# First projection of a hybrid encoder: blocks 1 to 5 as three products of split operands, with a group of loads moved on ScalarE's queue

## The chip, the cores and the metric

The program runs on one core of one Trainium2 chip. The metric is the device time of one execution in microseconds (us), median of several runs. TensorE (PE) multiplies, VectorE (DVE) and ScalarE (ACT) work element by element, GpSimd (POOL) does some of that too, and SyncE (SP) issues most transfers. Each engine works off its own instructions in order and meets the others at semaphores. A DMA that ACT issues takes time in ACT's own queue of instructions.

## What is computed

Two layers over T = 272 tokens (16 learned meta tokens and 256 given ones) of width 1024. The part that matters here is the start of layer 0:

```python
proj = rmsnorm(h, norm_mix_even[i]) @ w_in_ab[i]
ssd_out = ssd_mixer(proj[..., :o0], proj[..., o0:o1], proj[..., o1:o2],
                    ssd_conv_w[i], ssd_conv_b[i], ssd_a_log[i], ssd_dt_bias[i],
                    ssd_d[i], ssd_norm_w[i])
...
attn_out = diff_attention(proj[..., o2:], cos, sin, diff_lambda[i],
                          diff_subln_w[i], lambda_init)
h = h + jnp.concatenate([ssd_out, attn_out], axis=-1) @ w_out_ab[i]
```

In `ssd_mixer` a depthwise convolution over 5 tokens and a SiLU follow the projection, then a state-space scan in both directions. Behind it come a dense SwiGLU, a long convolution (Hyena) whose filter is a small network with sines, and a mixture of eight SwiGLU experts, which is most of the time.

## The kernel before

Everything is kept transposed: a tile is 128 output channels by 272 tokens in one of eight PSUM banks. The program has no scheduler. Each engine's instructions are written out by hand in their order, and `ORDER` numbers the PSUM tiles: a tile may be opened when the tile eight numbers before it has been read (`used_...`), and `tile_ready` counts the tiles that are closed.

The normalised input is `xn` (8 pieces of 128x272, fp32, written by DVE). The weights come in blocks of 256 columns (128x2048 numbers, 1 MB) through a ring of four slots. SP issues the first two at the start, and each later one when the last tile of the block four before it is closed. Block n of the projection gives tiles proj 2n and proj 2n+1. `linear` multiplies a block in plain fp32, 8 matmuls for each tile; the trace has two records for each such matmul.

PE's order is: blocks 0 (while `xn` comes), the transposed parameters, block 1, the 48 small matmuls of `dt`, blocks 2 and 3, filter layer 0 (`fw1`), block 4, filter layer 1 (`fw23`), block 5, filter layer 2, then cumulative sums (`cs`), transposes, and the head loop of the scan with blocks 6 to 9 in it. A filter layer k > 0 waits for the sine of layer k-1.

ACT copies each tile of blocks 0 to 3 to `xp`, applies the SiLU after the convolution (`ssd_silu`), and before tile 4 it takes the exp and log of `dt`. DVE makes one convolution for each of these eight tiles, 5 instructions (L1098, and L1034 four times), with the `dt` rows ahead of the fifth; then the arguments of the three sines (`filter_argument`, L1105 to L1110), which ACT's `filter_sine` (L707) waits for. From 85 us the head loop runs, in which DVE is busy without a pause.

Behind the input's transposes ACT issues five loads for `dt` and then eight more: the rest of the constant table `ktab`, `sel8` twice, `zpos`, `fw1`, `fw23` twice and the router. GpSimd's products W1 (L582) and DVE's masks need the table, PE's filter layers the small ones (`filter_in`).

Later stages (from the SwiGLU on, line 1236 and 815 for the splits) already use split operands: a number is x = hi + lo, with hi its copy rounded to fp32r (`ring_high` on ACT, `ring_low` on DVE for a block), and a product is three matmuls in fp32r:

```python
def product(o, hi, lo, moving, start, stop):
    mm(o, hi, moving[0], start, False)
    mm(o, hi, moving[1], False, False)
    return mm(o, lo, moving[0], False, stop)
```

Of the kernel before, what the change touches and what calls it, by code (L numbers as in the profile page):

```python
# [251 lines left out]
def trunk(nc, A, out):  # L252
    ctx = ExitStack()
    with ctx:
# [50 lines left out]
        ring_hi, ring_lo = overlay("ring_hi", 13600, 2, SLOT), overlay("ring_lo", arena_n, RING, SLOT)  # L305
        ring_hi2 = overlay("ring_hi2", 14864, 2, 256 * KT)
# [150 lines left out]

        def high_of(n, k):
            return ring_hi[:, n % 2, 0:256 * k] if n < B_HY else ring_hi2[:, (n + 1) % 2, 0:256 * k]

# [155 lines left out]
        def _(act):  # L616
# [57 lines left out]
            act.dma_start(ktab[:, K_FIRST:], A["k_table"][:, K_FIRST:]).then_inc(sem("table_in"), 16)  # L674
            for r in (0, 32):
                act.dma_start(sel8[r:r + HEADS, :], A["k_sel8"]).then_inc(sem("table_in"), 16)
            act.dma_start(zpos[:], A["k_zpos"]).then_inc(sem("filter_in"), 16)
            act.dma_start(fw1[:], A["hy_f_w1"][0]).then_inc(sem("filter_in"), 16)
            act.dma_start(fw23[:, 0, :], A["hy_f_w2"][0]).then_inc(sem("filter_in"), 16)
            act.dma_start(fw23[:, 1, :], A["hy_f_w3"][0]).then_inc(sem("filter_in"), 16)  # L680
            act.dma_start(router[:], A["moe_router"][0].rearrange("(k p) n -> p k n", p=P)).then_inc(sem("router_in"), 16)
# [8 lines left out]
            for j in range(8):  # L690
                if j == 4:

                    act.wait_ge(sem("dt_raw"), 1)
                    act.wait_ge(sem("dt_in"), 16 * 5)
                    a(nc.scalar.activation(dtw[:, 7, 0:16], a_log, ACT.Exp))
                    a(nc.scalar.activation(dtw[:, 2, :], dtw[:, 1, :], ACT.Exp, scale=-1.0))
                    a(nc.scalar.activation(dtw[:, 3, :], dtw[:, 2, :], ACT.Ln, bias=1.0), sem("dt_log"))
                copy("proj", j, xp[:, j, 2:2 + T])
                if j == 0:
                    parameters()  # L700
                if j >= 1:
                    ssd_silu(j - 1)
# [108 lines left out]

            def ring_high(n, i=0, k=KT):

                act.wait_ge(slot_in[n % RING], 16 * (n // RING + 1) + 16 * i)
                nc.scalar.activation(high_of(n, k), ring[:, n % RING, 0:256 * k], ACT.Copy).then_inc(sem("ring_high"), 1)  # L815

# [212 lines left out]
        def _(dve):  # L1029
# [37 lines left out]
            V.memset(crd[:, 7:8], 0.0).then_inc(used("ss1"), 1)  # L1067
            dve.wait_ge(used("param"), 1)
# [12 lines left out]
            for j in range(8):  # L1081
# [17 lines left out]
                for k in range(1, CONV):  # L1099
                    mult_add(c, xp[:, j, k:k + T], w(k), c, sem("conv_ready") if k == CONV - 1 else None)  # L1100
            def filter_argument(k):

                t = ready(dve, "mlp", k)
                x0, x1, x2 = harg[0:64, 0, :], harg[0:64, 1, :], harg[0:64, 2, :]
                v(V.tensor_scalar(x0, t[0:64, 0:ZT], par[0:64, C_FV + k:C_FV + k + 1], par[0:64, C_FV + 3 + k:C_FV + 4 + k], ALU.add, ALU.mult), used("mlp"))  # L1105
                v(V.tensor_scalar(x1, x0, 1.0 / (2.0 * math.pi), ROUND, ALU.mult, ALU.add))
                v(V.tensor_scalar(x1, x1, ROUND, None, ALU.subtract))
                mult_add(x0, x1, -TWO_PI_A, x0)
                mult_add(x2, x1, -TWO_PI_B, x0)
                v(V.tensor_scalar(x1, x2, 3.1415925, -3.1415925, ALU.min, ALU.max), sem("arg_ready"))  # L1110
# [120 lines left out]
            def ring_low(n, i=0, k=KT):  # L1231

                dve.wait_ge(sem("ring_high"), n - B_FF + 1 + 4 * i)
                c = slice(0, 256 * k)
                high = high_of(n, k)
                V.tensor_tensor(ring_lo[:, n % RING, c], ring[:, n % RING, c], high.bitcast(F32), ALU.subtract).then_inc(sem("ring_split"), 1)  # L1236

# [4 lines left out]
            def split_norm(col, s):  # L1242

                for k in range(KT + 1):
# [3 lines left out]
                    if k >= 1:  # L1248
                        dve.wait_ge(sem("xn_high"), KT + k)
                        V.tensor_tensor(xn_lo[:, k - 1, :], xn[:, k - 1, :], xn_hi[:, k - 1, :].bitcast(F32), ALU.subtract).then_inc(sem(s), 1)  # L1250

            def weighted_low(k, col):
                dve.wait_ge(sem("xn_high"), k + 1)
                V.scalar_tensor_tensor(out=xn_lo[:, k, :], in0=hT[:, k, :], scalar=par[:, col + k:col + k + 1], in1=xn_hi[:, k, :].bitcast(F32),
                                       op0=ALU.mult, op1=ALU.subtract).then_inc(sem("xn2_ready"), 1)
# [340 lines left out]
        def _(pe):  # L1596
# [25 lines left out]

            def turn(o, src, n=P):
# [71 lines left out]
            for n in range(6):  # L1695
                linear("proj", 2 * n, n, xn, coming=sem("xn1_ready") if n == 0 else None)
# [171 lines left out]
            def swiglu_columns(i, c, first=False):  # L1868

                for part in range(2):  # L1870
                    n = B_FF + 2 * c + part
                    pe.wait_ge(sem("ring_split"), 2 * c + part + 1 + 4 * i)
# [25 lines left out]
            for b in range(4):  # L1898
                for half in range(2):
                    n = B_DN + 2 * b + half  # L1900
                    pe.wait_ge(sem("ring_split"), n - B_FF + 1)
# [51 lines left out]
            def in_columns(i, b):  # L1953

                n = B_HY + b
                pe.wait_ge(sem("ring_split"), n - B_FF + 1 + 4 * i)
# [237 lines left out]
```

## Time and profile before

| | us |
|---|---|
| median of 3 runs (1646.52 to 1650.33) | 1646.89 |
| the profiled execution | 1656.01 |
| its span, first to last instruction | 1654.2 |
| PE busy in the span | 1614.9 (98%) |
| DVE busy | 1244.3 (75%) |
| ACT busy | 976.6 (59%) |

The profile is of one execution, which took 9.1 us more than the median of the runs. Busy times are sums over the span; which engine sets the end has to be read from the chain of waits and, for one stage, from the timelines of that stage. TensorE's clock has two levels, 1.2 and 2.4 GHz, and the column PEclk gives what was granted as a share of the higher one.

### The profile page before, as it was taken

What the parts mean: (1) busy time and instruction counts of PE and PEld (TensorE: products, weight loads), DVE (VectorE), ACT (ScalarE), POOL (GpSimd) and SP (SyncE); (2) the same over time, 40 slices, a digit from 0 to 9 for tenths busy, and PEclk for the clock granted to TensorE, in tenths of its full rate; (3) what the DMA queues carried; (4) which work ended last, traced back from release to release, by engine and by line L of the source; (5) the groups of instructions that cost most, each with busy time, mean ns of one, the idle gap of its engine ahead of it and who ended that gap; (6) DMA issues with size and microseconds to landing.
All of it is one profiled execution on the core that took longest, in us unless ns stands there. A gap on an engine that the chain in (4) does not pass through costs nothing.

```text
span 1654.2 us, 22043 instructions
## 1 busy us (share of the span) xinstructions
PE 1614.9 (98%) x8334; PEld 1350.9 (82%) x8334; DVE 1244.3 (75%) x1184; ACT 976.6 (59%) x885; POOL 77.7 (5%) x87
## 2 busy tenths in 40 slices
PE   8998999999999998999999999999999999999997
PEld 6765699999699587888888888888888888888886
DVE  5488456654647555988988888888888988988984
ACT  3274344433356124777677677677677677677773
POOL 0250000000302400000000000000000000000000
PEclk9999999999989997999999999999999999999998
DMA  8322145567125144999999999999999999999991
GB/s 279 102 79 75 48 143 170 174 195 213 52 86 169 52 153 141 372 375 332 355 370 339 356 370 340 356 372 337 356 372 337 357 373 336 355 375 332 355 369 66
DMA packets 221126, 429.60 MB, mean 260 GB/s; under 512 B 9514, under 2 KB 76592, under 8 KB 220752
## 3 DMA queue, kind: packets, MB, share of 16 engines
q1 hardware_dynamic: 217816, 424.82, 72.7%
q10 hardware_dynamic: 3256, 4.06, 0.7%
q8 instruction: 34, 0.56, 0.1%
q14 instruction: 20, 0.16, 0.0%
HBM read 427.80 MB, written 1.05 MB: 259 GB/s over the span
## 4 chain that ended last, share of the span: by engine, by line
PE 90%; DVE 5%; DMA 2%; ACT 1%; issue 1%; SPq 0%; DVEq 0%; ACTq 0%
PE ps L1612 87%; PE ps L1624 3%; DVE arena L1034 1%; DMA ring<-in_ffn_w_down_dram 1%; DMA raw<-in_moe_w_up_dram 1%; DVE arena L1137 0%; DVE ring_lo L1236 0%; DVE arena L1148 0%; DVE arena L1142 0%; DVE arena L1149 0%; ACT w_hi L925 0%; ACT ring_hi L815 0%; DMA raw<-in_moe_w_gate_dram 0%; DVE arena L1170 0%; DVE arena L1143 0%
## 5 line engine op out<-in xcount | busy, mean ns | idle before, releaser
L1400 DVE TENSOR_TENSOR w_lo<-raw,w_hi 128x2048 fp32r<-128x2048 f32 x224 | 511.9, 2290 | 82.4 <-ACT w_hi L925 81.4
L925 ACT ACTIVATE w_hi<-raw 128x2048 fp32r<-128x2048 f32 x224 | 429.3, 1919 | 182.0 <-DMA raw<-in_moe_w_up_dram 91.7
L1612 PE MATMUL ps<-w_hi,xg_hi 128*128 128x512 f32 x904 | 358.2, 396 | 4.7 <-DVE w_lo L1580 2.1
L1612 PE MATMUL ps<-w_hi,xg_lo 128*128 128x512 f32 x904 | 353.4, 391 | 0.0
L1612 PE MATMUL ps<-w_lo,xg_hi 128*128 128x512 f32 x904 | 352.7, 390 | 0.0
L1404 DVE TENSOR_TENSOR w_lo<-raw,w_hi 128x2048 fp32r<-128x2048 f32 x110 | 251.6, 2287 | 41.1 <-ACT w_hi L929 40.9
L929 ACT ACTIVATE w_hi<-raw 128x2048 fp32r<-128x2048 f32 x110 | 211.1, 1919 | 77.9 <-DMA raw<-in_moe_w_down_dram 77.5
L1612 PEld LDWEIGHTS ps<-w_hi,xg_hi 128*128 128x128 f32 x904 | 170.2, 188 | 39.3 <-DVE w_lo L1580 2.5
L1612 PEld LDWEIGHTS ps<-w_hi,xg_lo 128*128 128x128 f32 x904 | 169.9, 188 | 36.3
L1612 PEld LDWEIGHTS ps<-w_lo,xg_hi 128*128 128x128 f32 x904 | 170.4, 188 | 33.9
L1612 PE MATMUL ps<-w_hi,eh_hi 128*128 128x512 f32 x440 | 172.8, 393 | 1.7 <-issue 1.7
L1612 PE MATMUL ps<-w_lo,eh_hi 128*128 128x512 f32 x440 | 171.4, 390 | 0.0
L1612 PE MATMUL ps<-w_hi,eh_lo 128*128 128x512 f32 x440 | 171.4, 389 | 0.0
L1612 PE MATMUL ps<-xn_hi,ring_hi 128*128 128x272 f32 x544 | 159.1, 292 | 0.9 <-DVE crd L1348 0.8
L1612 PE MATMUL ps<-xn,ring 128*128 128x272 f32 (+1 forms) x640 | 158.8, 409 | 0.9 <-DVE xn L1034 0.8
L1612 PE MATMUL ps<-xn_hi,ring_lo 128*128 128x272 f32 x544 | 157.8, 290 | 0.0
L1612 PE MATMUL ps<-xn_lo,ring_hi 128*128 128x272 f32 x544 | 157.0, 289 | 0.0
L1236 DVE TENSOR_TENSOR ring_lo<-ring,ring_hi 128x2048 fp32r<-128x2048 f32 (+1 forms) x42 | 102.7, 2445 | 66.9 <-ACT ring_hi L815 66.0
L1612 PEld LDWEIGHTS ps<-xn,ring 128*128 128x128 f32 x640 | 126.8, 200 | 30.6 <-issue 5.3
L815 ACT ACTIVATE ring_hi<-ring 128x2048 fp32r<-128x2048 f32 (+1 forms) x42 | 85.6, 2038 | 72.6 <-PE ps L1612 59.9
L1612 PEld LDWEIGHTS ps<-xn_hi,ring_hi 128*128 128x128 f32 x544 | 103.0, 189 | 1.8 <-DVE crd L1348 0.9
L1612 PEld LDWEIGHTS ps<-xn_lo,ring_hi 128*128 128x128 f32 x544 | 103.1, 190 | 0.1
(289 smaller groups left out, 1920.1 us busy)
## 6 DMA issues: line engine op xcount, KB each, us to landing
raw<-in_moe_w_gate_dram SPq DMA_DIRECT2D x112, 1024.0 KB, 5.2
raw<-in_moe_w_up_dram SPq DMA_DIRECT2D x112, 1024.0 KB, 5.3
raw<-in_moe_w_down_dram SPq DMA_DIRECT2D x112, 1024.0 KB, 5.1
ring<-in_w_in_ab_dram SPq DMA_DIRECT2D x12, 1024.0 KB, 6.6
ring<-in_hy_w_in_dram SPq DMA_DIRECT2D x12, 1024.0 KB, 5.1
ring<-in_ffn_w_gate_dram SPq DMA_DIRECT2D x11, 1024.0 KB, 5.3
ring<-in_ffn_w_up_dram SPq DMA_DIRECT2D x11, 1024.0 KB, 5.3
ring<-in_ffn_w_down_dram SPq DMA_DIRECT2D x8, 1408.0 KB, 7.2
```

Source lines behind the costliest of these rows:

```text
L815: nc.scalar.activation(high_of(n, k), ring[:, n % RING, 0:256 * k], ACT.Copy).then_inc(sem("ring_high"), 1)
L925: nc.scalar.activation(w_hi[:, j, :], raw[:, j, :], ACT.Copy).then_inc(sem("gu_high"), 1)
L929: nc.scalar.activation(w_hi[:, 4 + j, :], raw[:, 4 + j, :], ACT.Copy).then_inc(sem("d_high"), 1)
L1034: v(V.scalar_tensor_tensor(out=out_, in0=in0, scalar=scalar, in1=in1, op0=op0, op1=op1), s)
L1236: V.tensor_tensor(ring_lo[:, n % RING, c], ring[:, n % RING, c], high.bitcast(F32), ALU.subtract).then_inc(sem("ring_split"), 1)
L1400: V.tensor_tensor(w_lo[:, j, :], raw[:, j, :], w_hi[:, j, :].bitcast(F32), ALU.subtract).then_inc(sem("gu_split"), 1)
L1404: V.tensor_tensor(w_lo[:, 4 + j, :], raw[:, 4 + j, :], w_hi[:, 4 + j, :].bitcast(F32), ALU.subtract).then_inc(sem("d_split"), 1)
L1612: return nc.tensor.matmul(o, l, r, start=start, stop=stop)
L1624: return nc.tensor.transpose(o, src, ident[0:n, 0:n])
```

## The change

Blocks 1 to 5 of the first projection are multiplied as three fp32r products instead of one fp32 product; block 0 stays as it is. For this ACT makes hi copies of the eight pieces of `xn` and of each block, and DVE the differences. The hi copies of blocks go to three buffers in turn (`ring_hi0`), the copies of `xn` to `xn0_hi` and `xn0_lo`. The copy and the difference of block 1 stand right behind those of `xn`; the copies of blocks 2 to 5 stand on ACT behind tiles 0, 2, 4 and 6, the differences on DVE behind convolutions 0, 2, 4 and 6. The eight later loads move on ACT's queue from ahead of the first tile's copy to behind the second tile's copy (`later_loads`). The counts of the semaphores that later stages share are adapted.

```diff
--- before.py
+++ after.py
@@ -303,6 +303,9 @@
         ring_hi, ring_lo = overlay("ring_hi", 13600, 2, SLOT), overlay("ring_lo", arena_n, RING, SLOT)
+        ring_hi0 = [overlay(f"ring_hi0{i}", at, 2048) for i, at in enumerate((5472, 7520, 20064))]
+        xn0_hi, xn0_lo = overlay("xn0_hi", 13056, KT, T), overlay("xn0_lo", 15232, KT, T)
         ring_hi2 = overlay("ring_hi2", 14864, 2, 256 * KT)
         ffh_hi, ffh_lo = overlay("ffh_hi", 0, FFT, T), overlay("ffh_lo", 5984, FFT, T)
         xn_hi, xn_lo = overlay("xn_hi", 19232, KT, T), overlay("xn_lo", 21408, KT, T)
@@ -455,8 +458,15 @@
                 return ("down", (n - B_DN) // 2 * 2 + (n - B_DN) % 2)
             return ("hy", 2 * (n - B_HY) + 1) if n < B_HO else ("ho", 2 * (n - B_HO) + 1)
+        EARLY = 5
         def high_of(n, k):
+            if n <= EARLY:
+                return ring_hi0[n % 3][:, 0:256 * k]
             return ring_hi[:, n % 2, 0:256 * k] if n < B_HY else ring_hi2[:, (n + 1) % 2, 0:256 * k]
+        def split_number(n):
+            return n if n <= EARLY else EARLY + n - B_FF + 1
         slot_in = [sem(f"slot{i}_in") for i in range(RING)]
@@ -671,14 +681,25 @@
             act.dma_start(a_log, A["ssd_a_log"].rearrange("e a h -> e (a h)").partition_broadcast(P)).then_inc(sem("dt_in"), 16)
             act.dma_start(lam_in, A["diff_lambda"].rearrange("e a h -> e (a h)").partition_broadcast(P)).then_inc(sem("dt_in"), 16)
             act.dma_start(d_in, A["ssd_d"].rearrange("e a h -> e (a h)").partition_broadcast(P)).then_inc(sem("dt_in"), 16)
-            act.dma_start(ktab[:, K_FIRST:], A["k_table"][:, K_FIRST:]).then_inc(sem("table_in"), 16)
-            for r in (0, 32):
-                act.dma_start(sel8[r:r + HEADS, :], A["k_sel8"]).then_inc(sem("table_in"), 16)
-            act.dma_start(zpos[:], A["k_zpos"]).then_inc(sem("filter_in"), 16)
-            act.dma_start(fw1[:], A["hy_f_w1"][0]).then_inc(sem("filter_in"), 16)
-            act.dma_start(fw23[:, 0, :], A["hy_f_w2"][0]).then_inc(sem("filter_in"), 16)
-            act.dma_start(fw23[:, 1, :], A["hy_f_w3"][0]).then_inc(sem("filter_in"), 16)
-            act.dma_start(router[:], A["moe_router"][0].rearrange("(k p) n -> p k n", p=P)).then_inc(sem("router_in"), 16)
+            def ring_high(n, i=0, k=KT):
+                act.wait_ge(slot_in[n % RING], 16 * (n // RING + 1) + 16 * i)
+                nc.scalar.activation(high_of(n, k), ring[:, n % RING, 0:256 * k], ACT.Copy).then_inc(sem("ring_high"), 1)
+            for k in range(KT):
+                act.wait_ge(sem("xn1_ready"), k + 1)
+                nc.scalar.activation(xn0_hi[:, k, :], xn[:, k, :], ACT.Copy).then_inc(sem("xn_high"), 1)
+            ring_high(1)
+            def later_loads():
+                act.dma_start(ktab[:, K_FIRST:], A["k_table"][:, K_FIRST:]).then_inc(sem("table_in"), 16)
+                for r in (0, 32):
+                    act.dma_start(sel8[r:r + HEADS, :], A["k_sel8"]).then_inc(sem("table_in"), 16)
+                act.dma_start(zpos[:], A["k_zpos"]).then_inc(sem("filter_in"), 16)
+                act.dma_start(fw1[:], A["hy_f_w1"][0]).then_inc(sem("filter_in"), 16)
+                act.dma_start(fw23[:, 0, :], A["hy_f_w2"][0]).then_inc(sem("filter_in"), 16)
+                act.dma_start(fw23[:, 1, :], A["hy_f_w3"][0]).then_inc(sem("filter_in"), 16)
+                act.dma_start(router[:], A["moe_router"][0].rearrange("(k p) n -> p k n", p=P)).then_inc(sem("router_in"), 16)
@@ -698,6 +719,15 @@
                 copy("proj", j, xp[:, j, 2:2 + T])
                 if j == 0:
                     parameters()
+                    ring_high(2)
+                if j == 1:
+                    later_loads()
+                if j in (2, 4, 6):
+                    n = 3 + (j - 2) // 2
+                    if n > 3:
+                        act.wait_ge(sem("tile_ready"), NUMBER[("proj", 2 * (n - 3) + 1)] + 1)
+                    ring_high(n)
                 if j >= 1:
                     ssd_silu(j - 1)
             ssd_silu(7)
@@ -1065,6 +1089,18 @@
             for k in range(KT):
                 mult_add(xn[:, k, :], t[:, 0:T], par[:, C_NME + k:C_NME + k + 1], hT[:, k, :], sem("xn1_ready"), ALU.mult, ALU.mult)
             V.memset(crd[:, 7:8], 0.0).then_inc(used("ss1"), 1)
+            def ring_low(n, i=0, k=KT):
+                dve.wait_ge(sem("ring_high"), split_number(n) + 4 * i)
+                c = slice(0, 256 * k)
+                high = high_of(n, k)
+                V.tensor_tensor(ring_lo[:, n % RING, c], ring[:, n % RING, c], high.bitcast(F32), ALU.subtract).then_inc(sem("ring_split"), 1)
+            for k in range(KT):
+                dve.wait_ge(sem("xn_high"), k + 1)
+                V.tensor_tensor(xn0_lo[:, k, :], xn[:, k, :], xn0_hi[:, k, :].bitcast(F32), ALU.subtract)
+            ring_low(1)
             dve.wait_ge(used("param"), 1)
             dve.wait_ge(sem("dt_in"), 16 * 5)
@@ -1098,6 +1134,8 @@
                 v(V.tensor_scalar(c, xp[:, j, 0:T], w(0), par[:, C_CB + j:C_CB + j + 1], ALU.mult, ALU.add))
                 for k in range(1, CONV):
                     mult_add(c, xp[:, j, k:k + T], w(k), c, sem("conv_ready") if k == CONV - 1 else None)
+                if j in (0, 2, 4, 6):
+                    ring_low(2 + j // 2)
             def filter_argument(k):
                 t = ready(dve, "mlp", k)
...
@@ -1620,6 +1651,16 @@
             def split_block(n, k=KT):
                 return [a.rearrange("p (k n) -> p k n", k=k) for a in (high_of(n, k), ring_lo[:, n % RING, 0:256 * k])]
+            def linear_split(group, j0, n):
+                pe.wait_ge(sem("ring_split"), split_number(n))
+                w_hi_, w_lo_ = split_block(n)
+                for j in range(2):
+                    o = open_tile(group, j0 + j)
+                    for k in range(KT):
+                        m = slice(P * j, P * j + P)
+                        last = product(o[:, 0:T], w_hi_[:, k, m], w_lo_[:, k, m], (xn0_hi[:, k, :], xn0_lo[:, k, :]), k == 0, k == KT - 1)
+                    close(last)
             def turn(o, src, n=P):
                 return nc.tensor.transpose(o, src, ident[0:n, 0:n])
@@ -1693,7 +1734,10 @@
                 close(mm(o[0:64, 0:ZT], fw23[:, k - 1, :] if k else fw1[:], harg[0:64, 3, :] if k else zpos[:]))
             for n in range(6):
-                linear("proj", 2 * n, n, xn, coming=sem("xn1_ready") if n == 0 else None)
+                if n == 0:
+                    linear("proj", 0, 0, xn, coming=sem("xn1_ready"))
+                else:
+                    linear_split("proj", 2 * n, n)
                 if n == 0:
                     parameters()
                 if n == 1:
...
```

On ACT, behind the five loads for `dt`, these rows stand before the change (L669 to L673 are those five; L624 copies a tile, L665 to L667 the parameters, L687 is the SiLU):

```order
L673 DMA bcast<-in_ssd_d_dram 128x16
L674 DMA ktab<-in_k_table_dram 128x6896
L676 DMA sel<-in_k_sel_dram 8x1024 x2
L677 DMA zpos<-in_k_zpos_dram 33x288
L678 DMA fw<-in_hy_f_w_dram 33x64
L679 DMA fw<-in_hy_f_w_dram 64x64
L680 DMA fw<-in_hy_f_w_dram 64x64
L681 DMA router<-in_moe_router_dram 128x8x8
L624 ACTIVATE arena<-ps 128x272 [waits tile_ready]
```

And at the same place of the changed kernel (L634 copies a tile, L687 is a block's hi copy there, L691 that of `xn`, printed by the names that share its address):

```order
L683 DMA bcast<-in_ssd_d_dram 128x16
L691 ACTIVATE xn_hi<-xn 128x272 [waits xn1_ready] x8
L687 ACTIVATE ring_hi<-ring 128x2048 [waits slot1_in]
L634 ACTIVATE arena<-ps 128x272 [waits tile_ready]
L675 ACTIVATE par<-ps 128x109 [waits tile_ready,used_proj]
L676 ACTIVATE par<-ps 128x112 [waits act_chain]
L677 ACTIVATE par<-ps 64x6 [waits act_chain]
L687 ACTIVATE ring_hi<-ring 128x2048 [waits slot2_in,used_param]
L634 ACTIVATE arena<-ps 128x272 [waits tile_ready]
L695 DMA ktab<-in_k_table_dram 128x6896 [waits used_proj]
```

The eight loads have moved behind two tiles' copies, the parameters and two hi copies of blocks.

On DVE, this is the part from the fifth convolution to the first filter argument before the change:

```order
L1098 TENSOR_SCALAR arena<-arena,par 128x272 [waits xbc_ready,used_proj,a_vec_ready]
L1034 SCALAR_TENSOR_TENSOR arena<-arena,par 128x272 [waits dve_chain] x4
L1098 TENSOR_SCALAR arena<-arena,par 128x272 [waits xbc_ready,used_proj,conv_ready]
L1034 SCALAR_TENSOR_TENSOR arena<-arena,par 128x272 [waits dve_chain] x4
L1098 TENSOR_SCALAR arena<-arena,par 128x272 [waits xbc_ready,used_proj,conv_ready]
L1034 SCALAR_TENSOR_TENSOR arena<-arena,par 128x272 [waits dve_chain] x4
L1098 TENSOR_SCALAR arena<-arena,par 128x272 [waits xbc_ready,used_proj,conv_ready]
L1034 SCALAR_TENSOR_TENSOR arena<-arena,par 128x272 [waits dve_chain] x4
L1105 TENSOR_SCALAR arena<-ps,par 64x288 [waits tile_ready,conv_ready]
```

And the same part of the changed kernel (L1134 and L1058 are the convolution, L1098 is a block's difference there):

```order
L1134 TENSOR_SCALAR arena<-arena,par 128x272 [waits xbc_ready,used_proj,a_vec_ready]
L1058 SCALAR_TENSOR_TENSOR arena<-arena,par 128x272 [waits dve_chain] x4
L1098 TENSOR_TENSOR ring_lo<-ring,ring_hi 128x2048 [waits ring_high,conv_ready]
L1134 TENSOR_SCALAR arena<-arena,par 128x272 [waits xbc_ready,used_proj]
L1058 SCALAR_TENSOR_TENSOR arena<-arena,par 128x272 [waits dve_chain] x4
L1134 TENSOR_SCALAR arena<-arena,par 128x272 [waits xbc_ready,used_proj,conv_ready]
L1058 SCALAR_TENSOR_TENSOR arena<-arena,par 128x272 [waits dve_chain] x4
L1098 TENSOR_TENSOR ring_lo<-ring,ring_hi 128x2048 [waits ring_high,conv_ready]
L1134 TENSOR_SCALAR arena<-arena,par 128x272 [waits xbc_ready,used_proj]
L1058 SCALAR_TENSOR_TENSOR arena<-arena,par 128x272 [waits dve_chain] x4
L1143 TENSOR_SCALAR arena<-ps,par 64x288 [waits tile_ready,conv_ready]
```

The differences of blocks 4 and 5 stand between the convolutions, ahead of the filter argument; those of blocks 2 and 3 stand in the same way between the first four. On PE the matmuls of blocks 1 to 5 wait for `ring_split`, the count of these differences, where they waited for the block's transfer.

## Rows read from the trace of the kernel before

**Rows 1.** The page: span, and the chain that ended last by engine.
```profile
span 1654.2 us, 22043 instructions
...
PE 90%; DVE 5%; DMA 2%; ACT 1%; issue 1%; SPq 0%; DVEq 0%; ACTq 0%
```

**Rows 2.** Timeline, PE: start us, us, instruction, shapes, count [idle before <- releaser].
```profile
24.83 7.60 PE L1612 MATMUL ps<-xn,ring 128*128 128x272 f32 x32
32.27 4.14 PE L1612 MATMUL ps<-wdt,xn 128*128 128x16 f32 x48
...
53.51 7.60 PE L1612 MATMUL ps<-xn,ring 128*128 128x272 f32 x32
61.04 0.69 PE L1612 MATMUL ps<-arena,fw 64*64 64x288 f32 x2
...
137.32 1.74 PE L1612 MATMUL ps<-arena 128*64 128x272 f32 x12 [2.22 <-DVE arena L1034]
```

**Rows 3.** Windows: stretch, length, busy PE, PEld, DVE, ACT, POOL, PEclk, DMA, GB/s.
```profile
14.00:20.00 6.00, 5.99 (x13) 4.52 (x14) 3.46 (x8) 0.00 (x0) 0.00 (x0) 1.00 0.60 165
14.00:122.00 108.00, 107.99 (x504) 82.18 (x505) 66.71 (x134) 49.52 (x103) 31.88 (x28) 0.95 0.45 144
31.00:37.00 6.00, 6.00 (x58) 5.63 (x57) 5.61 (x12) 2.22 (x6) 0.00 (x0) 1.00 1.17 318
...
126.00:129.00 3.00, 3.00 (x9) 2.20 (x8) 2.83 (x6) 2.31 (x6) 0.00 (x0) 0.50 0.29 101
```

**Rows 4.** Timeline, ACT and the DMA issues in its queue.
```profile
14.92 0.49 ACTq L674 DMA_DIRECT2D ktab<-in_k_table_dram  x1
...
18.78 0.67 ACTq L681 DMA_DIRECT2D router<-in_moe_router_dram  x1
20.94 0.40 ACT L624 ACTIVATE arena<-ps 128x272 f32<-128x272 f32 x1 [8.64 <-PE ps L1612]
...
58.79 0.44 ACT L707 ACTIVATE arena<-arena 64x288 f32<-64x288 f32 x1 [2.15 <-DVE arena L1110]
...
85.29 6.17 ACT L736 ACTIVATE arena<-ps,arena 128x272 f32<-128x272 f32 x12 [0.27 <-PE ps L1612]
```

**Rows 5.** Timeline, DVE.
```profile
13.36 4.25 DVE L1034 SCALAR_TENSOR_TENSOR xn<-ps,par,hT 128x272 f32<-128x272 f32 x8 [1.44 <-PE ps L1612]
...
27.20 0.42 DVE L1098 TENSOR_SCALAR arena<-arena,par 128x272 f32<-128x272 f32 x1
27.66 2.11 DVE L1034 SCALAR_TENSOR_TENSOR arena<-arena,par 128x272 f32<-128x272 f32 x4
...
37.63 0.17 DVE L1085 TENSOR_TENSOR arena<-ps,bcast 128x16 f32<-128x16 f32 x1
...
41.96 0.94 DVE L1034 SCALAR_TENSOR_TENSOR arena<-arena 128x48 f32<-128x48 f32 x4 [3.51 <-ACT arena L697]
...
43.54 2.40 DVE L1034 SCALAR_TENSOR_TENSOR arena<-arena,par 128x272 f32<-128x272 f32 x4
...
56.15 0.57 DVE L1105 TENSOR_SCALAR arena<-ps,par 64x288 f32<-64x288 f32 x1
```

**Rows 6.** Timeline, PE in the SwiGLU stage: first and last of 57 split matmuls.
```profile
299.79 0.29 PE L1612 MATMUL ps<-xn_hi,ring_hi 128*128 128x272 f32 x1
...
306.84 0.29 PE L1612 MATMUL ps<-xn_hi,ring_lo 128*128 128x272 f32 x1
```

**Rows 7.** Groups of instructions by form: count, busy us, mean ns, idle before.
```profile
L1236 DVE TENSOR_TENSOR ring_lo<-ring,ring_hi 128x2048 fp32r<-128x2048 f32 x34 | 77.9, 2292 | 39.3 <-ACT ring_hi L815 38.5
L815 ACT ACTIVATE ring_hi<-ring 128x2048 fp32r<-128x2048 f32 x34 | 65.2, 1916 | 35.0 <-PE ps L1612 31.2 <-DMA ring<-in_ffn_w_up_dram 1.9 <-DMA ring<-in_ffn_w_gate_dram 0.3
...
L835 ACT ACTIVATE xn_hi<-xn 128x272 fp32r<-128x272 f32 x8 | 3.4, 430 | 5.0 <-DVE xn L1246 5.0
```

**Rows 8.** Timeline, GpSimd.
```profile
42.38 6.79 POOL L582 TENSOR_SCALAR arena<-ktab,arena 128x272 f32<-128x272 f32 x6 [40.83 <-DVE arena L1034]
```

**Rows 9.** DMA issues of the first 130 us, with size.
```profile
ktab<-in_k_table_dram ACTq DMA_DIRECT2D x1, 3448.0 KB
```

More of the change, by code:

```diff
@@ L810, in squares @@
                 a(nc.scalar.activation(sq[:, k, toks], hT[:, k, toks], ACT.Square), sem(s))
-            def ring_high(n, i=0, k=KT):
-                act.wait_ge(slot_in[n % RING], 16 * (n // RING + 1) + 16 * i)
-                nc.scalar.activation(high_of(n, k), ring[:, n % RING, 0:256 * k], ACT.Copy).then_inc(sem("ring_high"), 1)
             def weighted_high(k, col):
@@ L1229, in _ @@
                 V.memset(crd[:, 8:9], 0.0).then_inc(used("nb"), 1)
[L1231 to L1236, printed above, removed]
             def add_to_stream(group, j):
@@ L1248, in split_norm @@
                     if k >= 1:
-                        dve.wait_ge(sem("xn_high"), KT + k)
+                        dve.wait_ge(sem("xn_high"), 2 * KT + k)
                         V.tensor_tensor(xn_lo[:, k - 1, :], xn[:, k - 1, :], xn_hi[:, k - 1, :].bitcast(F32), ALU.subtract).then_inc(sem(s), 1)
             def weighted_low(k, col):
-                dve.wait_ge(sem("xn_high"), k + 1)
+                dve.wait_ge(sem("xn_high"), KT + k + 1)
                 V.scalar_tensor_tensor(out=xn_lo[:, k, :], in0=hT[:, k, :], scalar=par[:, col + k:col + k + 1], in1=xn_hi[:, k, :].bitcast(F32),
@@ L1871, in swiglu_columns @@
                     n = B_FF + 2 * c + part
-                    pe.wait_ge(sem("ring_split"), 2 * c + part + 1 + 4 * i)
+                    pe.wait_ge(sem("ring_split"), split_number(n) + 4 * i)
                     w_hi_, w_lo_ = split_block(n)
@@ L1900, in _ @@
                     n = B_DN + 2 * b + half
-                    pe.wait_ge(sem("ring_split"), n - B_FF + 1)
+                    pe.wait_ge(sem("ring_split"), split_number(n))
                     w_hi_, w_lo_ = split_block(n, 11)
@@ L1955, in in_columns @@
                 n = B_HY + b
-                pe.wait_ge(sem("ring_split"), n - B_FF + 1 + 4 * i)
+                pe.wait_ge(sem("ring_split"), split_number(n) + 4 * i)
                 w_hi_, w_lo_ = split_block(n)
```

## Prediction, written before the result was known

> **What bounds the kernel now.** I read the page first: the program occupies 1654.2 us of a 1656.0 us execution, and TensorE is 90% of the chain that ended last [rows 1]. The change touches only the front end, up to the fused loads, so I then read that stretch engine by engine. TensorE (PE) has no idle time between 14.0 and 122 us: the rows of PE's timeline follow each other [rows 2], and the windows say the same, 107.99 us busy in 14:122 [rows 3]. So any time PE saves before about 85 us comes off the end, and any time PE is made to wait there is added to it. Around 88 us the chain goes over to VectorE (DVE), but what starts that part is a PE tile, so it shifts with PE.
>
> What the reader should see in the other timelines is who PE does *not* wait for now, and by how much. The second filter layer on PE (fw2, line 1612) needs the first sine of ScalarE (ACT). That sine starts at 58.79 and ends at 59.23 [rows 4]; PE asks for it at 61.04 [rows 2]. That is a slack of 1.8 us, and it is the smallest one near the change. The sine follows DVE's filter argument, which starts at 56.15, right behind the eighth convolution of DVE [rows 5]: 2.6 us from there to the sine's start.
>
> **The change, part by part.**
>
> *Products.* A plain fp32 block is 16 matmuls (two records each, so x32) and takes 7.53 us, 53.51 to 61.04 [rows 2]; 0.2 of that is the last one's drain, the rest 0.229 per record. A split block needs 48 matmuls, and these start every 0.126 us: 56 steps from 299.79 to 306.84 [rows 6]. With the same drain that is 6.05 + 0.2 = 6.24 us. Five blocks gain 5 x 1.29 = 6.4 us on PE, if nothing keeps PE waiting.
>
> *Splits of the input and block 1.* ACT is free at 14.92 [rows 4], because the eight later loads are gone from there. Eight copies of 0.43 us [rows 7], the last one after DVE's last xn (13.36 + 4.25 = 17.6 [rows 5]), end at 18.6; the 1.92 us copy of block 1 ends at 20.5, ahead of ACT's first tile copy at 20.94 [rows 4]. DVE's eight differences of about 0.43 us start at 17.7 and end at 21.4, block 1's takes 2.29 us and ends at 23.8. PE asks for it at 24.83, and DVE's first convolution starts at 27.20 in any case, after the parameters. Cost 0; the cover is 1.1 us.
>
> *Splits of blocks 2 to 5.* Four copies on ACT (1.92 us) and four differences on DVE (2.29 us, with the gap 2.32) [rows 7] go between the convolutions. A convolution takes 2.57 us (27.20 to 27.66 + 2.11 [rows 5]), with the gap 2.61. DVE's own queue, worked out from there: convolution 0 ends at 29.8, difference 2 at 32.1, convolutions 1 and 2 at 37.5, difference 3 at 39.8, convolution 3 at 42.4, the dt rows at 43.25 (37.63 to 38.45, 0.82). Now DVE waits for ACT's exp and log as before, 3.51 us [rows 5], to 46.75; four small rows (0.94) to 47.7; convolution 4, with 0.45 for GpSimd, to 50.8; **difference 4 to 53.1**; convolutions 5 and 6 to 58.3; difference 5 to 60.6; convolution 7 to 63.2; argument 0 (2.6) to 65.8; the sine to 66.3. So the idle time that DVE has now between convolutions 4 to 7 (about 1 us each) is filled (the sum has none left), and the queue becomes the bound.
>
> *What PE meets.* Block 1 runs 24.83 to 31.0, dt (4.1 us [rows 2]) to 35.2, block 2 to about 42.7 with the half-clock stretch that follows dt today too, block 3 to 48.9, layer 0 to 49.5 (0.6, the gap from 61.04 to block 5). Then PE waits for difference 4 until 53.1, 3.6 us. Block 4 ends at about 59.3. Then it waits for the first sine: layer 1 starts at **66.35 instead of 61.04, +5.3 us**. Queued behind it are block 5, layer 2 and everything after. Block 5 gives back 7.53 - 6.24 = 1.3. The gains of blocks 1 to 4 are all spent in the two waits. Sum so far **+4.0 us**.
>
> *The clock.* After idle or light work PE's records run at half speed: 13 records in 14:20, where the full rate gives 26, so 5.6 us at the lower rate lose 2.6 us, though the granted column says 1.00 there; and in 126:129 the granted clock is 0.50 (1.2 of 2.4 GHz) [rows 3]; those 3 us lose 1.5. Before layer 1 PE would sit idle for about 7 us, longer than any idle of it in the front end. I expect block 5 to start at half clock and take 2.2 us, between the two rows and nearer the first, since the idle is nearer to that case; bounds 0 and 3. Block 4 may be slowed too, but the wait behind it hides that. The Trainium skill (TensorE: Matmul & The Clock Gate, "What's actually happening") says "the default state is throttled, and activity releases the throttle": it speaks against this change, which trades array time for idle time, and the trace agrees in 14:20.
>
> *GpSimd alongside.* Its six W1 rows (6.8 us from 42.38 [rows 8]) move to about 47 to 54 and lie beside convolution 4 and difference 4. Beside them four convolution rows take 2.40 instead of 2.11 now [rows 5], and the first one of five 0.15 more. For a 2.29 us difference no row shows it; the nearest bounds are 0 and one GpSimd row, 1.1 us. I take 0.0 beyond the 0.45 on the convolution and keep 1.1 for the range. The Trainium skill (SBUF — State Buffer, "SBUF: two separate sides") calls that port pair an exclusive lock held for a whole instruction; taken at its word that is the upper bound here. No row here shows a full block of a long difference.
>
> *The later loads.* All eight issues move from 14.92 to 19.45 (4.5 us of ACT's queue [rows 4]) to behind ACT's second tile copy, 28.2 to 32.7. Behind them stand the first SiLU with its table load, tile 2's copy and block 3's copy. The SiLU ends at 34.4 and tile 2's copy at 34.9, where DVE wants them at 34.7: 0.1 us, and DVE's queue of splits is the cover; without it some 4 us. They include the large table, 3448 KB [rows 9]. At the 318 GB/s of 31:37 [rows 3] it and one more block need some 15 us, so the small loads behind it on that queue land near 44. PE needs them at 48.9 and difference 4 covers up to 52.5. Cost 0. The bandwidth freed at 15 to 28 only brings blocks 2 and 3 earlier, and nobody waits for these today. SP's queue keeps its order.
>
> **Sum:** +5.3 for the wait, -1.3 for block 5, +2.2 for the clock: +6.2 us, so the profiled execution's 1656.0 would become 1662.2, and the median of the runs, 1646.9 (9.1 under it), **1653.1 us**. About 0.3% (4.9 us) is what a measurement of this kernel tells from no change.
>
> **Rivals.** (A) As above, 1651 to 1656: 0.50. (B) The wait is there, but PE's clock does not suffer, or DVE's queue is a us shorter than summed: +4.0 and down to +2, about 1650: 0.28. For it: the rows from 137.32 on run at full rate after an idle of 2.22 us (12 in 1.74 us [rows 2]). Against: the idle here is three times that. (C) Waits add up: GpSimd holds difference 4 for 1.1 us and a further half-clock stretch like that of 126:129 falls into the light matmuls behind layer 2; 1.1 + 0.8 (the clock at its bound) + 1.5 on top, 1656.5: 0.12. (D) On the other side, faster: PE does not wait, because DVE keeps up. The place is the first sine. It decides at the point where layer 1 starts before 62.3 (61.04 plus block 5's 1.3), so DVE's queue would have to be 4 us shorter than the sum. The price is up to -6.4, 1640.5 us. For it speaks only that DVE has idle time between its convolutions now; the sum has used that up. 0.04. (E) The whole effect is soaked up later, because the DVE-bound part after 88 us does not shift: about 1647. Against it: that part starts on a PE tile. 0.06.
>
> **How the numbers follow.** The time is that of A. Slower by over 0.3% needs more than +4.9: nine tenths of A, C, and a little of B, 0.6. Faster is D, 0.04. The rest, 0.36, is no change. The range leaves out D and the far ends: from B's lower part, 1648, to a little past C, 1657.5.
>
> **What would show it.** In the changed profile: PE split tiles every 3.0 us at full clock; a PE idle before block 4 released by DVE's ring_lo near 53; a larger one before fw2 released by ACT's sine near 66; block 5's records at about 560 instead of 290 ns or with a granted clock of 0.5; table and small loads landed before 49; the decay rows of ACT that start the DVE part at 85.29 now [rows 4] near 91. I am wrong if PE shows no idle before fw2, if the idle there is under 4 us, or if the loads land after 53 and PE waits for them.

## The result and the profile after

| | kernel before | changed kernel |
|---|---|---|
| median, us | 1650.07 (20 runs) | 1655.60 (20 runs) |
| range of the runs, without one run of before that took 4853 us | 1641.56 to 1656.56 | 1649.64 to 1664.58 |
| profiled execution, us | 1656.01 | 1651.07 |
| its span, us | 1654.2 | 1649.2 |

The ratio is 1.0033, with a 95% interval of 1.0017 to 1.0049: the change makes the kernel slower by 5.5 us, 2.8 to 8.1. Predicted were +6.2 us. (The prediction's 1653.1 us counts from 1646.9, the median of three runs; over 20 runs the kernel before has 1650.07, so the two changes are compared here, not the two times.) The two profiled executions lie on the far sides of their medians, so their spans say the opposite; the comparison has to be made in the stretch that the change touches. I use one measure for it in all runs, **the front end**: from PE's rows for the parameters (24.41 us before, right ahead of block 1) to ACT's first decay rows (85.29 [rows 4]). It was 60.9 us before. Time 0 of a trace shifts against the work by up to 3 us (the parameter rows stand at 21.34 us in a second profile of the same kernel), in part because block 0 runs at the lower clock for a varying time; this measure leaves that out.

The timeline of PE in the changed kernel (start, us, instruction, count, idle before and its releaser):

```profile
23.05 0.49 PE L1665 MATMUL ps<-ktab,prow 117*128 117x117 f32 x3
...
45.99 0.70 PE L1643 MATMUL ps<-zpos,fw 33*64 33x288 f32 x2
51.63 0.59 PE L1643 MATMUL ps<-xn_hi,ring_hi 128*128 128x272 f32 x1 [4.94 <-DVE ring_lo L1098]
65.03 1.19 PE L1643 MATMUL ps<-arena,fw 64*64 64x288 f32 x2 [5.43 <-ACT arena L737]
66.15 0.59 PE L1643 MATMUL ps<-xn_hi,ring_hi 128*128 128x272 f32 x1
...
73.66 0.69 PE L1643 MATMUL ps<-arena,fw 64*64 64x288 f32 x2
```

Where [rows 2] show PE going through without a pause, there are now two waits: 4.94 us before block 4, ended by DVE's difference, and 5.43 us before filter layer 1, ended by ACT's sine. The timelines of DVE and ACT show what is behind the second:

```profile
45.09 0.94 DVE L1058 SCALAR_TENSOR_TENSOR arena<-arena 128x48 f32<-128x48 f32 x4 [3.52 <-ACT arena L718]
46.06 0.57 DVE L1134 TENSOR_SCALAR arena<-arena,par 128x272 f32<-128x272 f32 x1
46.67 2.41 DVE L1058 SCALAR_TENSOR_TENSOR arena<-arena,par 128x272 f32<-128x272 f32 x4
49.11 2.46 DVE L1098 TENSOR_TENSOR ring_lo<-ring,ring_hi 128x2048 fp32r<-128x2048 f32 x1
...
56.99 2.29 DVE L1098 TENSOR_TENSOR ring_lo<-ring,ring_hi 128x2048 fp32r<-128x2048 f32 x1
...
61.80 0.57 DVE L1143 TENSOR_SCALAR arena<-ps,par 64x288 f32<-64x288 f32 x1
```

```profile
64.44 0.44 ACT L737 ACTIVATE arena<-arena 64x288 f32<-64x288 f32 x1 [2.15 <-DVE arena L1148]
...
89.76 6.18 ACT L766 ACTIVATE arena<-ps,arena 128x272 f32<-128x272 f32 x12 [0.26 <-PE ps L1643]
```

Behind the wait for ACT's log (3.52 us, as before) DVE has no idle time left up to the first argument (compare [rows 5]); the argument starts 38.75 us after PE's parameter rows, where it was 31.74. So four differences of 2.3 us moved it by 7.0 us; the rest went into what was idle time. The windows of this stretch (length, busy PE, PEld, DVE, ACT, POOL, PEclk, DMA share, GB/s) show the clock and the end of the moved loads:

```profile
45.00:46.00 1.00, 1.00 (x10) 0.85 (x8) 0.81 (x4) 0.95 (x2) 0.49 (x1) 1.00 0.09 32
46.00:52.00 6.00, 1.06 (x4) 0.56 (x4) 5.79 (x8) 5.84 (x7) 5.63 (x5) 0.71 0.57 175
52.00:56.00 4.00, 4.00 (x21) 4.00 (x21) 3.72 (x9) 1.21 (x3) 1.36 (x2) 0.58 0.00 0
...
65.00:69.00 4.00, 3.97 (x14) 3.14 (x15) 2.38 (x6) 0.74 (x3) 0.00 (x0) 0.50 0.00 0
69.00:73.00 4.00, 4.00 (x34) 4.00 (x33) 0.00 (x0) 0.81 (x2) 0.00 (x0) 1.00 0.02 4
```

After each wait the granted clock is at or near 1.2 GHz (0.58 and 0.50) for some us, and PE starts 21 and 14 matmuls in 4 us instead of 34. The loads are through at 45 us, 22 us after the parameter rows. Nobody waits for them, but filter layer 0 starts at 45.99, so the margin was 1 us. The front end is 89.76 - 23.05 = 66.7 us, 5.8 more than before. That this is so near to the 5.5 us between the medians is in part chance: a second pair of profiles gives 67.1 and 59.4, 7.7 us.

### The profile page after: what moved, and what is told of

Read it like the earlier page. It is cut to its first block, busy times and chain, and to the rows that moved or that the text cites. A ratio compares the mean times of both kernels' runs of the same rounds, so it can differ in the third digit from the quotient of the medians.

```text
span 1649.2 us, 22239 instructions
## 1 busy us (share of the span) xinstructions
PE 1601.3 (97%) x8414; PEld 1347.7 (82%) x8414; DVE 1258.7 (76%) x1197; ACT 989.7 (60%) x898; POOL 78.9 (5%) x87
## 4 chain that ended last, share of the span: by engine, by line
PE 89%; DVE 7%; ACT 2%; DMA 1%; issue 1%; ACTq 0%; SPq 0%; DVEq 0%
PE ps L1643 86%; PE ps L1665 3%; DVE arena L1058 2%; DMA ring<-in_ffn_w_down_dram 1%; ACT ring_hi L687 0%; DVE arena L1175 0%; DVE ring_lo L1098 0%; DVE arena L1186 0%; DVE arena L1180 0%; DVE arena L1187 0%; DMA raw<-in_moe_w_gate_dram 0%; DVE arena L1208 0%; DMA ktab<-in_k_table_dram 0%; DVE arena L1176 0%; DVE arena L1181 0%
## 5 line engine op out<-in xcount | busy, mean ns | idle before, releaser
L1643 PE MATMUL ps<-xn_hi,ring_hi 128*128 128x272 f32 x624 | 184.8, 296 | 5.9 <-DVE ring_lo L1098 4.9
L1643 PE MATMUL ps<-xn_hi,ring_lo 128*128 128x272 f32 x624 | 182.8, 293 | 0.0
L1643 PE MATMUL ps<-xn_lo,ring_hi 128*128 128x272 f32 x624 | 182.0, 292 | 0.0
L1098 DVE TENSOR_TENSOR ring_lo<-ring,ring_hi 128x2048 fp32r<-128x2048 f32 (+1 forms) x47 | 114.3, 2432 | 66.7 <-ACT ring_hi L687 65.2
L687 ACT ACTIVATE ring_hi<-ring 128x2048 fp32r<-128x2048 f32 (+1 forms) x47 | 95.2, 2026 | 72.5 <-PE ps L1643 60.2
L1643 PEld LDWEIGHTS ps<-xn_hi,ring_hi 128*128 128x128 f32 x624 | 120.1, 193 | 8.2 <-DVE ring_lo L1098 5.4
L1643 PEld LDWEIGHTS ps<-xn_lo,ring_hi 128*128 128x128 f32 x624 | 120.3, 193 | 0.1
L1643 PEld LDWEIGHTS ps<-xn_hi,ring_lo 128*128 128x128 f32 x624 | 119.9, 192 | 0.0
L1643 PE MATMUL ps<-xn,ring 128*128 128x272 f32 (+1 forms) x480 | 115.5, 400 | 0.9 <-DVE xn L1058 0.8
```

The source lines that it names most:

```text
L1643: return nc.tensor.matmul(o, l, r, start=start, stop=stop)
```

## Experiments

The twelve runs, in one table; "wait 4" and "wait L1" are PE's idle time before block 4 and before filter layer 1, the clock is the mean granted share over the timed runs. The runs were made in three groups, each on another chip (e1 to e4; e5 to e8; e9 to e12), and each ratio is to runs of the kernel before on the same chip. One run of e9, which took 3224 us, is left out.

| run | front end | wait 4 | wait L1 | ratio to before [95%] | clock |
|---|---|---|---|---|---|
| before | 60.9 | 0 | 0 | 1 | 0.978 |
| e9, before again | 59.4 | 0 | 0 | 0.9996 [0.9975, 1.0018] | 0.978 |
| changed | 66.7 | 4.9 | 5.4 | 1.0033 [1.0017, 1.0049] | 0.973 |
| e8, changed again | 67.1 | 2.0 | 5.6 | 1.0035 [1.0018, 1.0052] | 0.972 |
| e1, layers behind block 5 | 61.1 | 3.3 | 0 | 1.0018 [1.0003, 1.0033] | 0.973 |
| e2, block 4 in the gap | 63.2 | 0 | 8.4 | 1.0016 [1.0002, 1.0030] | 0.975 |
| e3, PE kept busy | 66.3 | 0.7 | 2.5 | 1.0062 [1.0042, 1.0082] | 0.975 |
| e4, all in place | 55.2 | 0 | 0 | 1.0025 [1.0011, 1.0039] | 0.971 |
| e10, the same again | 57.8 | 0 | 0 | 0.9998 [0.9976, 1.0021] | 0.972 |
| e5, loads first | 73.7 | 4.8 | 4.9 | 1.0088 [1.0057, 1.0119] | 0.970 |
| e6, three blocks | 62.8 | 0 | 4.6 | 1.0030 [1.0012, 1.0048] | 0.973 |
| e7, only the loads | 59.5 | 0 | 0 | 1.0005 [0.9986, 1.0024] | 0.979 |
| e11, only the order | 64.2 | 0 | 0 | 1.0066 [1.0042, 1.0090] | 0.970 |
| e12, layers and gap | 61.2 | 0 | 2.0 | 0.9981 [0.9959, 1.0003] | 0.974 |

**e8 and e9, the two kernels again.**

> The changed kernel once more on the same chip as the three others, as their yardstick. Expected: ratio 1.003 as measured, front end 66.7 us, waits of about 4.9 and 5.4 us before block 4 and layer 1.

> The kernel before, unchanged, as a second profile of it. It tells how far the length of the front end and of the rest differ between two executions of one program. Theory (the front end is set by waits and varies only with the half-clock stretches): front end 60 to 62 us, ratio 1.000. Rival (a front end of 60.9 was an odd execution): more than 2 us away from it.

The front ends repeat within 0.4 and 1.5 us, with half-clock stretches in other places; e9's 59.4 is a little under its range. In e8 one came with the dt matmuls (granted clock 0.53 in 32:36, 1.00 in the changed kernel's first profile), so PE was later at block 4 and waited 2.0 us instead of the expected 4.9, and the front end stayed: the two waits don't add up, the second takes in the first. A front end taken from one profile is good to some 1.5 us. Behind it the spread is larger: from the decay rows to the first split copy of the SwiGLU stage it is 112.4 and 109.1 us in the two profiles of before, 109.1 and 113.0 in the two of the changed kernel.

**e1, the wait for the sine taken away by order.**

```diff
-    add("proj", 8, 2)
+    add("proj", 8, 4)
     add("mlp", 1)
-    add("proj", 10, 2)
-    add("mlp", 2)
     add("cs", 0, 3)
+    add("mlp", 2)
```

with PE's calls of `filter_layer(1)` behind block 5 and `filter_layer(2)` behind the `cs` tiles.

> The changed kernel with filter layer 1 put behind block 5 on PE and layer 2 behind the cumulative sums; splits as in the change. Measure: length of the front end, from PE's parameter rows to ACT's first decay row, 60.9 us before and 66.7 changed. Theory (VectorE's queue makes PE wait twice, at block 4 and at the first sine): the wait of 5.4 us before layer 1 goes, the 4.9 us before block 4 stays, block 5 runs at full clock; front end 59 to 61, time about that of the kernel before or 1 us under it. Rival (the cost is in the split products or the clock, not in that wait): the wait turns up elsewhere, front end 65 to 67, time +5 us.

PE's timeline:

```profile
50.27 0.60 PE L1642 MATMUL ps<-xn_hi,ring_hi 128*128 128x272 f32 x1 [3.34 <-DVE ring_lo L1097]
64.22 0.70 PE L1642 MATMUL ps<-arena,fw 64*64 64x288 f32 x2
```

The wait at block 4 is still there, the one for the sine is gone, and the front end is back at 61.1. So DVE's queue reached the front end's end through the first sine. The time came down by less than expected, to +3.0 us (0.5 to 5.4 with its interval, which overlaps that of the changed kernel). Where these 3 us are is not shown; e11 below shows that moving the layers behind block 5 has a price of its own.

**e2, block 4's split in DVE's and ACT's gap.**

```diff
                 if j == 4:
+                    act.wait_ge(sem("tile_ready"), NUMBER[("proj", 3)] + 1)
+                    ring_high(4)
...
                     mult_add(dtw[:, 1, :], dtw[:, 0, :], -1.0, dtw[:, 0, :], sem("dt_raw"), ALU.mult, ALU.max)
+                    ring_low(4)
                     dve.wait_ge(sem("dt_log"), 1)
```

with the two calls gone from behind tile and convolution 4.

> The changed kernel with the hi copy of block 4 ahead of ACT's exp of dt and its difference in the 3.5 us in which VectorE waits for ACT's log. Theory (the first sine decides, and the wait at block 4 is covered by it): PE's 4.9 us wait before block 4 vanishes, but the time falls only by what VectorE's queue gets shorter, 2.3 us: front end 64.4, time +3 us over before; PE's wait before layer 1 grows to some 10 us. Rival (the two waits add up): front end 61.8, time +0.5 us.

```profile
61.30 1.19 PE L1646 MATMUL ps<-arena,fw 64*64 64x288 f32 x2 [8.37 <-ACT arena L739]
```

A wait of 4.9 us was removed, and the one behind it grew from 5.4 to 8.4. What the end gained is what DVE's queue lost, as the theory has it; it lost 3.7 us instead of 2.3. ACT's timeline says where the other 1.3 comes from: with block 4's copy ahead of it, the table load for exp no longer comes behind the wait for `dt`, as it did in the changed kernel at 41.64.

```profile
38.33 1.28 ACT L718 ACT_TABLE_LOAD   x1
41.53 0.22 ACT L718 ACTIVATE arena<-bcast 128x16 f32<-128x16 f32 x1 [1.92 <-DVE arena L1060]
```

**e6, three blocks.** `EARLY = 3`; blocks 4 and 5 stay with `linear`, and their copies and differences are gone.

> Only blocks 1 to 3 are split; 4 and 5 stay plain fp32, so two differences (4.6 us) leave VectorE's queue ahead of the first sine. Theory (queue of VectorE): no wait before block 4, the first sine about 4.6 us earlier than in the changed kernel, layer 1 about 0.7 us later than before, block 5 7.5 us; front end 61 to 63 us, time 0 to +2 us over before. Rival (the split products themselves cost time in proportion to the blocks): three fifths of the change's +5.5, front end 64.4, time +3.3 us.

No wait at block 4, layer 1 at 58.85 us (37.3 after the parameter rows; 36.6 before, 42.0 in the changed kernel). That is the 0.7 us of the theory. The front end is in its range; the time, +5 us with an interval of 2 to 8, is above it and closer to the rival's, so e6 by its time alone settles nothing.

**e5, the loads at their old place.** `later_loads()` is called ahead of the copies of `xn`.

> The changed kernel with the eight later loads at their old place, ahead of the splits of the input. Theory (moving them costs nothing, and leaving them would put the splits of xn and block 1 about 4 us later on ACT): block 1's difference ends near 27 instead of 22.3 after the same start, PE waits some 3 us before block 1, VectorE's queue starts 1 to 2 us later, and only that shows at the end: front end 68 us, time +1 to +1.5 us over the changed kernel. Rival (the moved loads are part of the cost of the change): front end under 66, time below the changed kernel by 1 us or more.

Both theories missed: front end 73.7 us, +14.5 us in time. The wait before block 1 is there as expected (2.16 us), but it is ACT's timeline that shows the price:

```profile
32.88 1.91 ACT L698 ACTIVATE ring_hi<-ring 128x2048 fp32r<-128x2048 f32 x1 [8.53 <-DMA ring<-in_w_in_ab_dram]
```

ACT waits 8.5 us for block 2 itself. With the 3448 KB table [rows 9] on its way first, block 2 lands only at 32.8 us. Before the change PE asked for it at 36.34; ACT's copy wants it at 24.4. In the changed kernel the same copy runs at 24.43 without a wait. So with the early splits the move of the loads is worth 7 us of front end and 9 us of time (+14.5 against +5.5).

**e7, only the loads moved** (the kernel before, `later_loads()` behind the second tile's copy).

> The kernel before with the eight later loads behind the second tile's copy and nothing else. Theory: nothing waits for them and ACT has the room; front end 60.9, time as before within 1 us. Rival (the small loads behind the table come too late for layer 0, or the first SiLU holds VectorE's queue): a wait of PE before layer 0 or layer 1, time +1 us or more.

Nobody waits, the front end is 59.5, as in e9. Alone the move shows no change (-2.3 to +4.0 us).

**e3, PE kept busy.**

```diff
+            def keep_busy(o, count):
+                for k in range(count):
+                    mm(o[:, 0:T], high_of(3, KT)[:, 256 * (k % KT):256 * (k % KT) + P], xn0_hi[:, k % KT, :])
+
             def linear_split(group, j0, n):
+                if n == 4:
+                    keep_busy(open_tile(group, j0), 32)
```

and 36 of them ahead of layer 1's wait.

> The changed kernel with 32 and 36 additional matmuls, whose results are overwritten, ahead of the waits for block 4's difference and for the first sine. Theory (2.2 us of the cost is block 5 and layer 1 at half clock after the idle): granted clock 1.00 in block 5, which takes 6.2 instead of 8.0 us; front end 64.5, time +3 us. Rival (the clock falls for another reason, or costs nothing): front end 66.7 or more, time +5 us.

```profile
52.00:62.00 10.00, 10.00 (x82) 10.00 (x81) 9.50 (x16) 1.79 (x5) 1.22 (x2) 1.00 0.31 96
62.00:65.00 3.00, 0.50 (x4) 0.25 (x3) 2.03 (x6) 0.82 (x3) 0.00 (x0) 1.00 0.11 34
65.00:68.00 3.00, 3.00 (x14) 2.58 (x13) 2.23 (x6) 0.56 (x2) 0.00 (x0) 0.62 0.00 0
```

The filling took away the half-clock stretch of block 4 (52:62 at 1.00) but not that of block 5: 2.5 us of idle were left, and the clock was down from 65 on for some 3 us all the same. Layer 1 and block 5 together take 8.4 us (8.6 in the changed kernel), not 6.9. So this run doesn't separate the clock's share from the wait's, and its +10 us in time are not explained by its front end of 66.3. That stays open.

**e4 and e10, all in place.** e2's edit; block 5's copy and difference one convolution earlier (`j == 5`); on PE layer 1 between the second and the third `cs` tile and layer 2 behind the third.

> The changed kernel with block 4's split in the dt gap, block 5's difference one convolution earlier, layer 1 behind the first two cumulative sums and layer 2 behind the third. Theory (with no wait in PE's way the products give their 6.4 us): PE idle under 2 us before block 5 and none else, front end 54 to 56, time 1643 to 1646 against 1650 before, ratio 0.996 to 0.998. Rival (three products with their splits do not pay on this stretch): front end 60 or more, ratio 1.000 or above.

> The version with the splits in DVE's gaps once more, since its front end was 5.7 us shorter than before and its time 4 us longer. Theory (the gain is given back as half-clock time of TensorE in the stages behind): front end again 54 to 57 us, mean granted clock again near 0.971 against 0.978 before, time +2 to +5 us. Rival (the first measurement was an accident): clock as before and time 3 to 6 us under before.

The front end does what the theory says: no wait of PE before any block or layer, 55.2 and 57.8 us, on the mean 3.6 us less than in the two profiles of before. The time doesn't follow. In e4 it is +4.1 us (1.8 to 6.4), where -4 to -7 were expected. In e10 it is no change by the ratio (-4.0 to +3.5 us, though its median lies 3.4 above), where +2 to +5 were expected. So the gain of the front end shows in neither time. From the decay rows to the first split copy of the SwiGLU stage it is 114.9 and 115.0 us here against the 112.4 and 109.1 of before, and the mean clock over the timed runs is 0.971 and 0.972.

**e11, only PE's order** (the kernel before, all blocks plain, with the order of e4).

> The kernel before with only PE's order of that version: filter layer 1 behind the first two cumulative sums, layer 2 behind the third, all blocks plain fp32. If the clock behind the front end is lost through this order (more light matmuls in a row), the mean granted clock is near 0.972 and the time +3 us or more; if it is lost through the split products, clock and time are those of before (0.978, within 2 us) and the front end is 60 to 62 us.

This was the run that told it apart, and against the split products: the order alone costs 10.9 us by the ratio (6.9 to 14.8; 12.3 between the medians) and the clock falls to 0.970. Against e9's profile, e11's front end is 4.8 us longer, the stretch from there to the SwiGLU stage 6.2 us (115.3 against 109.1), and what follows is no longer. The windows of e11, from its cumulative sums on:

```profile
66.00:71.00 5.00, 5.00 (x24) 2.03 (x23) 0.89 (x3) 0.00 (x0) 0.00 (x0) 1.00 0.67 210
71.00:85.00 14.00, 13.08 (x53) 9.05 (x53) 5.35 (x13) 5.97 (x15) 2.88 (x3) 0.51 0.00 1
...
122.00:200.00 78.00, 68.69 (x296) 43.12 (x295) 53.38 (x122) 32.88 (x82) 5.54 (x6) 0.87 0.13 41
```

and the last window in the two profiles of the kernel before:

```profile
122.00:200.00 78.00, 68.56 (x309) 43.99 (x308) 53.44 (x123) 32.87 (x83) 4.24 (x5) 0.93 0.13 41
122.00:200.00 78.00, 70.44 (x328) 47.77 (x327) 52.57 (x121) 32.56 (x79) 1.58 (x2) 0.98 0.17 56
```

These windows hold somewhat different work, since e11's front end ends later. Laid over the same 476 matmul records, from the decay rows to the split copy, the granted clock is 0.91 in e11 and 0.95 and 0.98 in the two profiles of before: part of this difference is there between two executions of one program. The small products follow each other for 20.6 us in e11 (66.11 to 86.66), 14 of them at half clock, with 0.9 us of waiting. In the two profiles of before they take 16.1 and 14.9 us, about 7 and 3 of them at half clock. Layer 1 (0.6 us) is the only work that has joined them; layers 1 and 2 now stand between the sums, and block 5 ahead of all of them. Which of this brings the clock down is not shown. Against e11, with the same order on PE, the splits of e4 and e10 gain 7 and 11 us by the ratios: in that setting three products do pay.

**e12, splits in the gaps, layer 1 ahead of all sums** (e1's order with e4's splits).

> Splits in VectorE's gaps as in the version with all in place, but PE's order as in the run with the layers behind block 5: layer 1 ahead of the cumulative sums, where it waits for the sine. Theory (queue): PE waits about 2 us for the sine at 62.5, front end 57 to 59 us. If the time follows the front end alone it is 2 to 3 us under before; if split blocks cost granted clock behind them, it is 2 to 5 us above before with a clock near 0.972.

PE waits 1.99 us for the sine, as expected. The front end of this profile, 61.2, is above the range, with 14 us of small products (66:80) at a clock of 0.58; the profiled execution took 1656.09 us, the longest of the 12. The median is the lowest of the changed versions, 1646.9 against 1648.4, ratio 0.9981; the interval reaches 1.0003. It may be 3 us faster than before and can't be told from no change.

## Why the prediction was right

**The queue of DVE** was the step on which everything rested, and it held to a few tenths. Counted from PE's parameter rows the difference of block 4 was to end at 28.7 (53.1 - 24.41) and ended at 28.5 (51.57 - 23.05); the first sine at 41.9 and 41.8; layer 1 was to start 5.3 us later than before and started 5.35 later (5.27 in e8). e1, e2 and e6 change that queue or who waits for it, and the front end follows each time.

**The wait at block 4** was sized 3.6 and measured 4.9. The end of the wait was right; PE came to it 1.4 us earlier than summed, because no half-clock stretch followed the dt matmuls in this execution. In e8 one did, and the wait was 2.0. It changed nothing, since the wait for the sine lies behind it. That second wait was to be about 7 us and was 5.43, because block 4 ran partly at half clock (51.63 to 59.6, 8.0 us instead of 6.2), which the prediction had allowed for.

**Block 5 and the clock.** Layer 1 and block 5 took 8.63 us (65.03 to 73.66) where [rows 2] and the profile before have 8.16. The prediction had -1.3 for the products and +2.2 for the clock, +0.9; measured is +0.5, so the clock cost 1.8 (2.2 in e8, 1.9 in e2). That it fell after a long idle is shown in all three. That idle alone is the cause is not: e3 removed over half of the idle before layer 1 and kept 1.5 us of the loss, and in the kernel before the clock was down to 0.57 with PE busy all the time. The Trainium skill's sentence that activity releases the throttle (TensorE: Matmul & The Clock Gate, "What's actually happening") fits 52:62 of e3, where the filling held the clock. The window of before, over the small products:

```profile
74.00:82.00 8.00, 8.00 (x46) 7.17 (x45) 0.15 (x1) 2.21 (x6) 2.88 (x3) 0.57 0.01 2
```

**GpSimd alongside.** Its six rows took 7.9 us instead of 6.8 and the difference beside them 2.46 instead of 2.29: 0.2 us, near the lower bound of 0. For DVE the block of a whole instruction, the upper bound, did not happen. For GpSimd something near it did: the row that starts at 50.00, beside the difference (49.11 to 51.57), took 2.40 us where the median of the six is 1.03 and the longest before the change was 1.22. e1, e3, e5 and e8, with the same difference beside these rows, show one such row of 2.4 us each; e2, e4, e6, e10 and e12, where the difference stands elsewhere or is gone, show none over 1.2. Nobody waited for that row here.

**The moved loads** cost nothing, as said. Counted from the parameter rows they landed at 22 where 19.6 was worked out, and PE needed them at 22.9 instead of 24.5: the margin of some 5 us was 1 us. The sentence that nobody waits for blocks 2 and 3 holds for the kernel before, but it leaves out the changed kernel, where ACT's copy wants block 2 at 24.4: e5 shows ACT waiting 8.5 us for it if the table goes first. The prediction didn't need that number, since the move was part of the change.

**The sum**: +5.8 us of front end and +5.5 us of time, +6.2 predicted. The mechanism was the predicted one. That all three lie within a us is partly luck: over both pairs of profiles the front end grew by 6.8 us on the mean, and the interval of the time is 2.8 to 8.1.

## What to carry to other kernels

A cheaper product on the busiest engine pays only as far as the engines that prepare it have room ahead of the next thing that engine waits for. Work out the preparing engine's queue to that point, instruction by instruction; here it had 1.8 us of slack and got four differences of 2.3 us. When a wait is removed, look who waits next and at the half-clock stretches behind: a front end 3.6 us shorter came with no shorter time. A table of 3.4 MB that nobody needs soon belongs behind the 1 MB blocks that somebody does.

## What the runs showed of the hardware that was not expected

- The order of small matmuls alone moved the mean granted clock of the whole program from 0.978 to 0.970 and the time by 11 us (e11), with no instruction added or removed. Why the stretch from the decay rows to the SwiGLU stage is slower too (115.3 us), where the order is the old one, these runs don't settle: e1 and e12, with one and the same order, nearly that of e11, had 110.7 and 115.3 us, and the two profiles of before differ by 3.3 us there.
- Where half-clock stretches fall differs between two executions of one program: right behind the dt matmuls in e8 (granted clock 0.53 in 32:36), not in the first profile of the same kernel (1.00).
- Half clock came after 2.50 us of idle in e3, not after 2.22 us in [rows 2]; but in e12 it came after 1.99 us, with small products behind (granted clock 0.50 in 61:66).
- With block 4's copy put ahead of the wait for `dt`, ACT's table load for exp ran at 38.33, 3.2 us ahead of its activation (e2); in the changed kernel it came at 41.64, only when the wait was over. That saved 1.3 us.
- One GpSimd row of 1.03 us took 2.40 us beside a 2.46 us difference of DVE, in five profiles out of five with that pair; the difference itself lost 0.17.
